# A two-layer encoder: gates, attention output and convolution output computed as rows of tokens, with a turn of the merged rows by TensorE

## What is computed

```
proj = u @ w_in[i]
y_conv = conformer_conv(proj[..., :c0], ...)          # its last step: y @ w_conv_out
y_attn = diff_attention(proj[..., c0:c1], ...) @ w_attn_out[i]
gates = jax.nn.sigmoid(proj[..., c3:])                # 2 * D_MODEL columns
merged = gates[..., :D_MODEL] * y_conv + gates[..., D_MODEL:] * y_attn
h = h + merged @ w_out[i]
...                                                   # cross attention, then a mixture of 32 experts
```

## Time and profile before

| | |
|---|---|
| median of 3 runs | 1781.58 us (1777.74 to 1784.85) |
| the profiled execution | 1784.98 us, of which the span in the profile is 1783.2 us |
| PE busy | 1508.3 us (85%) |
| DVE busy | 617.2 us (35%) |
| ACT busy | 528.4 us (30%) |
| DMA traffic | 530.86 MB |
| granted TensorE clock, mean | 0.941 of full speed |

### The profile page before, as it was taken

The page is one execution under the profiler, slowest core; times in us unless marked ns, Lnnn a source line. Parts: engine busy times, 40 slices in busy tenths (PEclk is TensorE's granted clock), DMA queues, the critical chain, the costliest instruction groups (busy, mean ns, idle before and its releaser), DMA issues.

```text
span 1783.2 us, 24289 instructions
## 1 busy us (share of the span) xinstructions
PE 1508.3 (85%) x9704; PEld 1013.6 (57%) x9704; DVE 617.2 (35%) x1020; ACT 528.4 (30%) x829; POOL 57.2 (3%) x100
## 2 busy tenths in 40 slices
PE   8999999999867676767699999999988768676776
PEld 7788889886323232323277878998853323232322
DVE  5556777653100010101054668775520101010101
ACT  6435654543200000000163465635431000000001
POOL 3011000000000000000000200000000000000000
PEclk8999999999998898988899999999989989888989
DMA  8536335754999999999955453457469999999997
GB/s 229 189 123 207 104 134 189 282 190 192 374 422 422 422 421 422 422 422 422 418 189 182 125 180 117 136 195 284 161 266 388 422 421 422 422 422 422 422 422 306
DMA packets 118162, 530.86 MB, mean 298 GB/s; under 512 B 8809, under 2 KB 9001, under 8 KB 68935
## 3 DMA queue, kind: packets, MB, share of 16 engines
q1 hardware_dynamic: 114944, 524.13, 74.1%
q0 software_dynamic: 3136, 5.73, 1.6%
q10 hardware_dynamic: 12, 0.05, 0.0%
HBM read 524.63 MB, written 1.05 MB: 295 GB/s over the span
## 4 chain that ended last, share of the span: by engine, by line
PE 57%; DMA 34%; DVE 3%; ACT 2%; SPq 2%; issue 2%; PEldq 0%; DVEq 0%; ACTq 0%
DMA ring<-in_w_dram 34%; PE ps L1981 10%; PE ps L1631 7%; PE ps L1636 7%; PE ps L1632 6%; PE ps L1665 5%; PE ps L1666 5%; PE ps L1671 5%; SPq L557 2%; PE ps L1713 2%; PE ps L2013 1%; PE ps L1965 1%; PE ps L1770 1%; PE ps L1793 1%; PE ps L1582 1%
## 5 line engine op out<-in xcount | busy, mean ns | idle before, releaser
L1981 PE MATMUL ps<-ring,big 128*32 128x512 f32 x2048 | 284.8, 708 | 146.9 <-DMA ring<-in_w_dram 119.2
L1116 DVE TENSOR_TENSOR weight_split<-ring,weight_split 128x1024 fp32r<-128x1024 f32 x224 | 271.0, 1223 | 171.7 <-ACT weight_split L730 168.8
L730 ACT ACTIVATE weight_split<-ring 128x1024 fp32r<-128x1024 f32 x224 | 234.6, 1058 | 224.8 <-PE ps L1671 94.7
L1981 PEld LDWEIGHTS ps<-ring,big 128*32 128x32 f32 x2048 | 81.3, 127 | 328.1 <-issue 327.9
L1631 PE MATMUL ps<-operand_split,weight_split 128*128 128x256 f32 x896 | 229.6, 293 | 2.6 <-DVE operand_split L1181 1.8
L1632 PE MATMUL ps<-operand_split,weight_split 128*128 128x256 f32 x896 | 220.5, 283 | 0.0
L1508 DVE TENSOR_TENSOR big<-big,ps 128x256 f32<-128x256 f32 x32 | 13.5, 421 | 489.1 <-ACT big L1008 489.1
L1631 PEld LDWEIGHTS ps<-operand_split,weight_split 128*128 128x128 f32 x896 | 171.7, 192 | 17.4 <-issue 14.6
L1632 PEld LDWEIGHTS ps<-operand_split,weight_split 128*128 128x128 f32 x896 | 171.9, 192 | 2.0 <-issue 1.9
L2013 PE MATMUL ps<-ring,big 128*32 128x512 f32 x1024 | 133.5, 659 | 35.3 <-DVE big L1508 30.9
L1665 PE MATMUL ps<-weight_split,operand_split 128*128 128x512 f32 x384 | 154.2, 402 | 4.8 <-issue 4.8
(11 more groups left out here) (243 smaller groups left out, 1436.6 us busy)
## 6 DMA issues: line engine op xcount, KB each, us to landing
ring<-in_w_dram SPq DMA_DIRECT2D x376, 1024.0 KB, 17.9
ring<-in_w_in_dram SPq DMA_DIRECT2D x28, 2048.0 KB, 7.9
ring<-in_w_xkv_dram SPq DMA_DIRECT2D x8, 2048.0 KB, 8.1
ring<-in_w_attn_out_dram SPq DMA_DIRECT2D x4, 2048.0 KB, 8.1
ring<-in_w_conv_out_dram SPq DMA_DIRECT2D x4, 2048.0 KB, 8.5
ring<-in_w_out_dram SPq DMA_DIRECT2D x4, 2048.0 KB, 8.8
big<-in_w_dram SPq DMA_DIRECT2D x8, 1024.0 KB, 14.6
ring<-in_w_xq_dram SPq DMA_DIRECT2D x4, 2048.0 KB, 8.9
```

The source lines that it names most:

```text
L730: act.activation(split_quarter(k, 0), landed_quarter(k), ACT.Copy).then_inc(w_hi, 1)
L1116: dve.tensor_tensor(split_quarter(k, 1), landed_quarter(k), split_quarter(k, 0).bitcast(F32), ALU.subtract).then_inc(w_lo, 1)
L1981: last = pe.matmul(ps[CAP * j:CAP * (j + 1), 1, :], xe[:, k, e * CAP:(e + 1) * CAP], pair_slot(j)[:, k, :], start=(k == 0), stop=(k == DC ...
```

## The change

The gate slabs and ao0, ao1, co0, co1 move to the row form. The gate tensors, `merged` and their products keep tokens on partitions. Since wo0 wants features on partitions, PE turns `merged` with 16 transposes per layer (jobs `mT0` to `mT3`, four each, banks 4 to 7); ACT rounds the turned bank into the high part, and DVE subtracts for the low part. The last quarter of a gate slab and of co1 is done tile by tile (`tile_quarter`), so that the first tile's bank is full before the second tile's products. In attention a gate slab takes its two banks in the first of four steps and gives them back by two copies in the last of the four.

```diff
-JOBS += ["xk.2"] + pairs("oT") + ["xk.3"] + pairs("ao.") + pairs("co.") + pairs("wo.")
+JOBS += ["xk.2"] + pairs("oT") + ["xk.3"] + pairs("ao.") + pairs("co.") + pairs("mT") + pairs("wo.")
...
-            return name[:-1] in ("a", "g", "v", "xv", "wo", "xo")
+            return name[:-1] in ("a", "g", "v", "gc", "ga", "ao", "co", "xv", "wo", "xo")
...
+                def merged_high(jobs):
+                    for j in jobs:
+                        act.wait_ge(*due(full[bank(f"mT{j}")], turn(f"mT{j}")))
+                        act.activation(m_s[0][:, 2 * j:2 * j + 2, :], ps[:, bank(f"mT{j}"), :].rearrange("p (c t) -> p c t", c=2),
+                                       ACT.Copy).then_inc(m_hi, 1)
+                split_to(QUARTERS * SLABS.index("wo0") + 1)
+                merged_high((0, 1))
+                split_to(QUARTERS * SLABS.index("wo0") + QUARTERS)
+                merged_high((2, 3))
...
-                    if s % 2 == 1:
-                        job = f"gate.{s // 2}"
-                        dve.wait_ge(*due(full[bank(job)], turn(job)))
-                        dve.tensor_copy(g[:, 2 * j:2 * j + 2, :], both(job)).then_inc(gate_raw, 1)
...
+                    if s % QUARTERS == QUARTERS - 1:
+                        for t in range(TT):
+                            n = s // QUARTERS * TT + t
+                            job = f"gate.{n}"
+                            dve.wait_ge(*due(full[bank(job)], turn(job)))
+                            dve.tensor_copy(g[:, t, half * SLAB:(half + 1) * SLAB], ps[:, bank(job), :]).then_inc(gate_raw, 1)
+                            dve.wait_ge(*due(gate_raw, n + 1))
+                            dve.sem_inc(free[bank(job)], 1)
...
+                def conv_gated(jobs):
+                    for j in jobs:
+                        job = f"co.{j}"
+                        dve.wait_ge(*due(full[bank(job)], turn(job)))
+                        g, m = at_rows(gate_c, j), at_rows(merged, j)
+                        ch.link(dve.tensor_tensor(g, ps[:, bank(job), :], g, ALU.mult))
+                        dve.sem_inc(free[bank(job)], 1)
+                        dve.tensor_tensor(m, m, g, ALU.add).then_inc(m_rows, 1)
...
+                low_ahead("co.1")
+                conv_gated((0, 1))
+                low_to(QUARTERS * SLABS.index("wo0") + 1)
+                merged_low((0, 1))
+                low_to(QUARTERS * SLABS.index("wo0") + 2)
+                conv_gated((2, 3))
+                low_to(QUARTERS * SLABS.index("wo0") + QUARTERS)
+                merged_low((2, 3))
...
+                def tile_quarter(kind, jobs, dst, q, xs):
+                    c = QUARTERS - 1
+                    hi, lo = split_quarter(q, 0), split_quarter(q, 1)
+                    pe.wait_ge(*due(w_hi, q + 1))
+                    for s in range(TT):
+                        for k in range(2):
+                            xh, xl = (d[:, 2 * c + k, s * P:(s + 1) * P] for d in xs)
+                            pe.matmul(dst[s], xh, hi[:, k, :], start=False, stop=False)
+                            pe.matmul(dst[s], xl, hi[:, k, :], start=False, stop=False)
+                        if s == 0:
+                            settle()
+                            pe.wait_ge(*due(w_lo, q + 1))
+                        for k in range(2):
+                            last = pe.matmul(dst[s], xs[0][:, 2 * c + k, s * P:(s + 1) * P], lo[:, k, :], start=False,
+                                             stop=(k == 1))
...
-                    if s % 2 == 0:
-                        gdst = begin(job)
-                    columns(gdst[:, (s % 2) * T:(s % 2 + 1) * T], QUARTERS * SLABS.index("gc0") + s, u_s,
-                            job if s % 2 else None)
+                    q = QUARTERS * SLABS.index("gc0") + s
+                    jobs = [s // QUARTERS * TT + t for t in range(TT)]
+                    if s % QUARTERS == 0:
+                        gdst = [begin(f"gate.{j}") for j in jobs]
+                    if s % QUARTERS == QUARTERS - 1:
+                        tile_quarter("gate.", jobs, gdst, q, u_s)
+                    else:
+                        row_quarter("gate.", jobs, gdst, q, s % QUARTERS, u_s)
...
+                def turn_merged(jobs):
+                    for j in jobs:
+                        pe.wait_ge(*due(m_rows, j // 2 * TT + TT))
+                        turn_rows(begin(f"mT{j}"), merged, j).then_inc(full[bank(f"mT{j}")], 1)
+                def after_co(c):
+                    if c == 1:
+                        turn_merged((0, 1))
+                def after_wo(c):
+                    if c == 0:
+                        turn_merged((2, 3))
...
-                col_jobs("ao.", "ao0", (0, 1), o_s)
...
+                row_jobs("ao.", "ao0", (0, 1), o_s, have=(lo_ready, DC, 1))
+                row_jobs("ao.", "ao1", (2, 3), o_s)
                 pe.wait_ge(*due(conv_lo_ready, 1))
...
+                row_jobs("co.", "co0", (0, 1), conv_s)
+                row_jobs("co.", "co1", (2, 3), conv_s, after_co, by_tile=True)
+                row_jobs("wo.", "wo0", (0, 1), m_s, after_wo, have=(merged_ready, 0, 1))
```

100 lines of the change are left out of this document (47 added, 53 removed).

## The result

The changed kernel is **slower by 0.2%**: 1784.53 us (median of 22 runs, 1779.43 to 1788.17) against 1779.60 of the kernel before in the same session (22 runs, 1773.07 to 1785.22); the ratio is 1.0023, 95% interval 1.0013 to 1.0033.

A forecast was written before the change was run, and what follows sets the result against it. Both touched stages were taken as bound by PE. Per layer +0.06 us in attention and -0.71 in the output projections, times two layers, made -1.3 us: 1780.3 us on the median of 1781.58, range 1774 to 1787.

The forecast's parts named there:

- Normal steps: Attention: a row-form gate quarter saves 0.16 us, so steps fall from 4.35 to 4.19; 13 steps gain 2.08 us per layer.
- Bank waits: Attention: PE waits 0.46 us for DVE's two gate copies, three times per layer (0.48 behind squares), 1.42 us in all.
- Restarts: Attention: the first product behind each of five new waits is 0.06 us longer, 0.30 us per layer.
- The two steps behind squares: Attention, steps 7 and 11: DVE's squares make the mix late, so PE waits 0.21 us at each turn, 0.42 per layer.
- Attention in all: Whole attention stage: the gates' gain is given back in full by the new waits, +0.06 us per layer.
- Projections: Output projections: 16 quarters gain 2.56 us, 16 transposes add 1.85, waits taken at 0; -0.71 us per layer.
- The second layer repeats the first; each term below counts twice.: Whole kernel: both layers gain or lose alike, so the per-layer sum is doubled to -1.3 us.
- the dense stage's gain arrives at the end one to one: Expert loop: its weights load into slots the dense stage frees, so it shifts as a whole by the dense stage's gain or loss.
- the clock falls: Rival, 5%: the five new waits per layer in attention each lower PE's clock, costing 14 us; 1794 us.
- all waits hidden: Rival, 17%: the new attention waits are covered, the stage keeps its 2.08 us per layer; -5.6 us, 1776.0 us.
- Attention bound by DVE in every step: Rival, 14%: attention steps stay near 4.3 us and the stage loses about 1.1 us per layer; +0.8 us, 1782.4 us.
- the row form saves nothing here: Rival, 4%: gate and projection quarters gain nothing, by a cited rule on product cost; +5.9 us, 1787.5 us.

The follow-up runs named there:

- e12: The changed kernel with PE's whole program 32 products further down, by small products at the very start: 1779.25 us, ratio 0.9996 to the kernel before.
- e16: The kernel before with PE's whole program 32 products further down, by small products at the very start: 1781.66 us, ratio 1.0002.
- e17: The kernel before with PE's whole program 56 products further down, by small products at the very start: 1782.30 us, ratio 1.0002.
- e9: The kernel before with 12 never-executed products in a branch behind the first layer's expert loop: 1783.78 us, ratio 1.0017.
- e7: The changed kernel with the second gate copy of each pair on ACT, each copy freeing its own bank: 1774.97 us, ratio 0.9967 to the kernel before.
- e14: e7 with PE's whole program 32 products further down, by small products at the start: 1770.44 us, ratio 0.9945 to the kernel before.
- e10: The changed kernel with 64 never-executed products (256 instructions) in a branch behind the first layer's expert loop: 1787.47 us, ratio 1.0036 to the kernel before.

## Why the prediction was wrong

**The sum for the touched stages came out small and negative, as forecast.** 2 x -0.2 = -0.4 us in the stages, -1.5 (-2.9 to 0.0) in the runs at comparable places; forecast -1.3. That -1.5 lies so near the forecast is luck: the stages give a third of it. By its terms, per layer:

- *Normal steps.* 4.24 us, not 4.19. The row quarter among other work takes 2.85, its first product 0.33 instead of 0.23; the 0.16 between back-to-back quarters was 0.12 here. Over 13 steps that is 0.6 us less gained.
- *Bank waits.* 0.46 to 0.47, three times, ended by the second copy, as worked out. PE went on 0.16 us behind that copy's end, where I had taken 0.06.
- *Restarts.* The 0.06 behind each wait were not there for the bank waits: 0.31 from 195.57 to 195.88, the same as the 0.33 from 190.80 of a quarter without a wait. The two steps behind squares cost 0.16 above a normal one, not 0.27.
- *Attention in all.* +0.37 (first scores to the turns of its output) against +0.06.
- *Projections.* -0.63 against -0.71, transposes without idle time. The waits there that I took at 0 were 0.

**What failed is the step "The second layer repeats the first; each term below counts twice."** The sentence ahead of it, that the dense stage's gain arrives at the end one to one, is not refuted. But the second layer's start is no copy of the first's: PE comes out of the expert loop into code that it has not fetched. In every profile of the changed kernel at its own place it waits there, 2.33 or 3.40 us, and start takes 22.3 to 22.5 us against 19.2 to 21.0 before, where the border falls late in the first quarter. Start also depends on when ACT begins its first split: some 2.1 to 2.6 us behind the last scatter's start, or 0.8 us at most. Compared within either group the wait lengthens start by 1.3 to 1.5 us (late) or 3.2 (early). This none of my terms nor rivals had. I read only the rows of stages that the diff touches.

**The rest is the clock, and only its size is shown.** e12 is 4.9 us below after, and start gives only 1.6 of that. In most profiles the granted clock falls to 0.50 for some 3 us, now and then for 7, behind some of the idle times outside the touched stages; each short fall costs 1.4 to 1.8 us, a long one twice that (first taps to first scores take 140.2, then 142.0, 143.7, 145.4). In the second layer up to those scores, after has three (at 898, 915 and 1031 us, the last a long one), before two (918 and 1034), e12, e16 and e17 none. The fall at 898 follows the wait for the program directly. That the later ones follow from it, because they fall at other moments, is argued, not shown: e9 has the wait and 140.19. The rival "the clock falls" had the mechanism at the wrong place: at the five new waits the clock stayed at 1.00.

**The rival "all waits hidden"** was not the changed kernel, yet e7 comes near to it, with the bank waits gone and those at the turns left: the rival gave 1776.0, and e7 has 1774.97. The agreement is partly luck. Its stage gains 1.6 to 1.8 us per layer over before, 3.4 in all, where the rival had 2.8 per layer; and it carries the wait at the second layer's start. What it has on top is the clock in routing, below.

**The other two rivals.** "Attention bound by DVE in every step" is refuted: a normal step is 4.24 us without idle time at its turn, where the rival had about 4.3, and attention lost 0.37 us, not 1.1. So is "the row form saves nothing here": steps fell from 4.35 to 4.24 and the projections by 0.63. The rule cited for it was not meant for this case: the section "Back-to-back issue gap" of "TensorE: Matmul & The Clock Gate" in the Trainium skill calls the formula that of an isolated product and gives other spacings for a stream of loads and products, which the prediction left out.

## What to carry to other kernels

A change of under 0.3% can't be judged at one code layout when the program leaves a loop for code not run yet: shift the whole program by a few tens of harmless instructions, in both versions, and compare at the places without a wait "issue" behind the jump. When two results used to be drained one by one and now come in pairs, give the second drain to the other engine; here the ratio to the kernel before went from 1.0023 to 0.9967 (e7), of which the stage itself explains a third, and with the shift by 32 to 0.9945 (e14, 5 runs, 1770.44 us, the fastest of this study). And read the seams between repeated stages, not only the stages that the diff touches.

## What the runs showed of the hardware

- Instructions that are never executed cost time: 48 of them (12 float32 products with their loads) behind a loop moved a wait to the jump's target and cost 2.9 us; 256 cost 3.0. At the program's start 32 to 224 more cost nothing or removed up to 5 us. The instruction queue moves 0.70 MB in 43 packets, 16 KB each. The section of the Trainium skill named above has a block hold 256 instructions, and the program's 64 bytes an instruction agree. I expected by it that e10's pad would put the border far off, but had counted 128 instructions where there are 256, a whole block.
- Behind a jump out of a loop, PE waited 3.5 to 3.8 us at the target if that lay two blocks behind the jump's, and not if it lay in the next one; for the block behind the target's it waited 0.6 to 3.4 us more where the border came within the first 20 products.
- From the end of the dense stage to the first expert's gather the six profiles with a copy on ACT take 17.24 to 17.26 us in 12 of 12 layers, without a fall of the clock; the fourteen others, with the same code there, take 17.23 to 17.26 in 6 of 28 layers and 18.1 or 19.8 in the rest, 18.95 in the mean. In both, PE idles 1.16 us at the same place ahead of it (after and e14). In the mean of the profiles this is worth 1.7 us per layer, 3.4 in all, as much as e7's dense stages gain; why the clock holds there I can't say.
- The cost of a clock fall is much the same wherever it comes: 140.2, 142.0, 143.7 and 145.4 us for one unchanged stage with none, one, two and three short falls, a long one counted as two.
